# Recurrent rounds of a two-block kernel: own places for the second round's rates and keys, the next preparation inside the inverse's steps, and decays as one exponential per direction

## The chip, the cores and the metric

One core of one Trainium2 chip runs the whole program. The metric is the device time of one execution in microseconds. Three executions of the kernel before gave 1541.13 us as their median (1539.18 to 1548.11).

## What is computed

Two blocks stand behind one another. The second, two transformer layers with three kinds of attention, isn't touched. The first block mixes pooling, a gated linear recurrence (HGRN) and an RWKV recurrence. The change lies in the RWKV part, which has 6 heads of 64 channels and two directions, over 256 context and 256 latent tokens:

```python
w_log = -softplus(-(w0[d] + tanh(xw) @ w_up[d])) - 0.5
decay = exp(-exp(w_log))                       # = exp(-DECAY * sigmoid(...)), DECAY = exp(-0.5)
a  = sigmoid(a0[d] + xa @ a_up[d])
kk = k * k_k;  kk = kk * rsqrt(sum(kk * kk) + 1e-12)
k_mod = k * (1 + (a - 1) * k_a)
...
sa = S @ kk_t                                  # one step of the scan, per head
S  = S * w_t - sa * (kk_t * a_t) + v_t * k_t
y  = S @ r_t
```

## The kernel before, in words

The program is written in Bass: each engine has its own instruction list, which it carries out in order, and semaphores tie the lists together. TensorE does the matmuls into PSUM, ScalarE (ACT in the rows) and VectorE (DVE) copy results out and do the elementwise work.

The scan isn't run token by token. 6 heads are taken as 3 **rounds** (`JT` = 3) of two heads, both directions together, in 4 chunks of 128 tokens. A round j has these parts, each a Python generator that every engine's list runs through in the same order of turns:

- **E, prepare** (`prepare_tensor` L876, `prepare_scalar` L1825, `prepare_vector` L2316): products for the rates (L883, `w` then `a`) and for the norm (L887), sigmoids (L1836) into `sw` and `la`, the sigmoids of HGRN's gates (L1850, L1851), the norm by Ln and Exp (L1857, L1860). VectorE sums the rates over each chunk (the scan L2325) and makes `km` (modified keys). ScalarE makes the decays as exponentials (L1867 to L1874), VectorE multiplies them into the keys `km` and rates `la` (L2354 to L2358).
- **S, scores** (L899, L1880, L2366): transposes of values, `km`, `la`; products of `la` with the queries `px`.
- **L, full tiles** (L965, L2389): four turns, `lk0`, `lk1`, `akb0`, `akb1`. TensorE multiplies `km` and `la` with `px` and `rl` (L973, L983), VectorE copies the result out under a mask (L2396).
- **I, inverse** (L988, L1951, L2400): 12 turns, six halvings l = 1 to 6 of two turns each. The first, called i1 to i6 here, is a product (L955; L962 for i6) whose result ScalarE copies out (L2001, one copy per direction). The second, x1 to x6, is a product (L955; L962 for x6) with, up to l = 5, its transposed form t1 to t5 (L946); VectorE copies these out (L2406; L2417 and L2426 for x6).
- **C, chain** (L1019, L1962, L2430): 8 turns, chunk by chunk: products rhs (L1030, L1034) and u (L1045), each copied by ScalarE, then s (L1053 to L1057), copied by VectorE (L2438). **Y** (L1060) reads the outputs.
- **H**, 12 turns of HGRN's work; **Q** and **N** (L1095, L1080), norms of HGRN's and RWKV's outputs; **T**, the rest of the input projection, ahead of the first round; **M**, the output projection, in the last.

The order of turns is written out by hand: `TAIL` (L239) and `order_of_streams` (L242). In a round's string each E is a turn of the *next* round's preparation. It lies in the second half of the inverse (i4 to x6) and in the chain:

```python
turns += list("SSS" + "ILHIHILHIHILHIHL")
if more:
    n = "N" if j else ""
    turns += list(f"IEQ{n}IEQ{n}IEQ{n}IEIEQ{n}EQ{n}IEQ{n}" + "CECHCHECHCHECHCHC" + "Y")
```

`la` and `km` have one place each for all rounds (L496), and S and L of round j read them. So `prepare_scalar` waits at L1828 for the product `akb1` of round j-1 and at L1829 for its transposes.

PSUM banks are handed out by `Pool` (L201) in the order of turns: a product waits until the last user of its bank has been copied out. The RWKV pool has 4 banks. What matters below: t3 takes the banks of `akb0`, and x4 those of `akb1`.

Of the kernel before, what the change touches and what calls it, by code (L numbers as in the profile page):

```python
# [18 lines left out]
ALU = mybir.AluOpType  # L19
# [219 lines left out]
TAIL = "TTETETTTTTTTTETTEETEHTETEHTHTHTETHTEH"  # L239

def order_of_streams():  # L242

    turns, steps = list(TAIL), []
    for j in range(JT):
        more = j + 1 < JT
        turns += list("SSS" + "ILHIHILHIHILHIHL")
        if more:
            n = "N" if j else ""
            turns += list(f"IEQ{n}IEQ{n}IEQ{n}IEIEQ{n}EQ{n}IEQ{n}" + "CECHCHECHCHECHCHC" + "Y")  # L250
        else:
            turns += list("IQNIQNIQNIQNQNIQNIM" + "CMCMCMCMCMCMCMCM" + "YMNNMNMNNMMMMN")
# [10 lines left out]
def run_streams(**streams):  # L263
# [124 lines left out]
def build(nc, a, out, first=True, second=True, dump=None):  # L388
# [3 lines left out]
    with ctx:  # L392
        sems = {}

        def sem(name):
            if name not in sems:
                sems[name] = ctx.enter_context(nc.semaphore(name))
            return sems[name]
# [60 lines left out]
        dmid, nmid, ecol = take(8, (2, 4)), take(8, (2, 4)), take(16, (2, 2, 4))  # L459
# [37 lines left out]
        nd, n6, xh, xth = [slots[0][:, n * 1024:(n + 1) * 1024].rearrange("p (d u t) -> p d u t", d=2, t=HALF) for n in range(4)]  # L497
        xf, lkm = [slots[2][:, n * 2048:(n + 1) * 2048].rearrange("p (d u t) -> p d u t", d=2, t=P) for n in range(2)]
# [377 lines left out]
        def prepare_tensor(pe, j, take_bank, turn):  # L876
# [12 lines left out]
            for _ in range(6):  # L889
                yield  # L890
# [934 lines left out]
        def prepare_scalar(act, j, copy, done, emptied):  # L1825

            if j:
                rw.wait_filled(act, f"akb1_{j - 1}")  # L1828
                ep.wait_filled(act, f"btok1_{j - 1}")  # L1829
# [11 lines left out]
            done("e_gates")  # L1841
            yield
# [19 lines left out]
            yield  # L1862
            for d in range(2):
                act.wait_ge(sem("e_cumulated"), 2 * j + d + 1)
                for c in range(4):
                    q = slice(c * P, (c + 1) * P)
                    act.activation(sw[:, d, q], sw[:, d, q], ACT.Exp, scale=-DECAY, bias=dmid[:, d, c:c + 1])  # L1867
                    if c >= 2:
                        act.activation(pl[:, d, (c - 2) * P:(c - 1) * P], cl[:, d, q], ACT.Exp, scale=-DECAY, bias=dmid[:, d, c:c + 1])
                act.activation(ecol[:, j % 2, d], ecol[:, j % 2, d], ACT.Exp)  # L1870
                act.drain()
                for c in range(4):
                    q = slice(c * P, (c + 1) * P)
                    act.activation(cl[:, d, q], cl[:, d, q], ACT.Exp, scale=DECAY, bias=nmid[:, d, c:c + 1])  # L1874
# [441 lines left out]
        def prepare_vector(dve, j, done, emptied, bc, fence):  # L2316
# [3 lines left out]
            k = us[:, 3 + j, :]  # L2320
            for d in range(2):
# [39 lines left out]
            yield  # L2361
# [645 lines left out]
```

## Time and profile before

| | before |
|---|---|
| median of 3 executions (lowest, highest) | 1541.13 us (1539.18, 1548.11) |
| the profiled execution, its time | 1543.86 us |
| its span in the profile | 1542.1 us |
| mean granted TensorE clock | 0.98 |
| TensorE busy | 1466.3 us (95%) |
| VectorE busy | 817.6 us (53%) |
| ScalarE busy | 336.7 us (22%) |

### The profile page before, as it was taken

To read this page: it belongs to the slowest core of one execution; us is meant where nothing else is said; L and a number is where in the kernel's file an instruction comes from. 1 tells how busy PE (TensorE), PEld (TensorE's weight loads), DVE (VectorE), ACT (ScalarE), POOL (GpSimd) and SP (SyncE) were. 2 spreads that over 40 slices of the span, in tenths; PEclk is the share of its full clock that TensorE was granted. 3 is DMA by queue.
4 is the path that set the end of the run, shared out by engine and by line. 5 is a ranking of instruction groups with operands and counts; after the bars stand their busy time and mean duration, and the time that the engine had idled before them with its cause. 6 is when DMAs were issued, how large, how long until landed. Compare 5 with 4: busy or idle time off the path is not lost.

```text
span 1542.1 us, 30923 instructions
## 1 busy us (share of the span) xinstructions
PE 1466.3 (95%) x13431; PEld 1277.7 (83%) x13431; DVE 817.6 (53%) x1497; ACT 336.7 (22%) x721; POOL 279.1 (18%) x144
## 2 busy tenths in 40 slices
PE   7999998889788989999999999999999999999998
PEld 2666857777677878998888999999999888899986
DVE  2342244565653258667622766534866743466653
ACT  1103132543532231033400121001104340012100
POOL 3403001000000018663200000002875320000000
PEclk9999999989799999999999999999999999999999
DMA  9313150000003246433344454454553324345451
GB/s 352 127 55 109 57 190 2 4 2 4 17 3 112 77 108 225 164 110 110 113 161 163 142 175 175 167 164 125 179 177 143 116 110 149 130 163 172 164 188 61
DMA packets 101239, 191.30 MB, mean 124 GB/s; under 512 B 8648, under 2 KB 17568, under 8 KB 100976
## 3 DMA queue, kind: packets, MB, share of 16 engines
q1 hardware_dynamic: 99728, 187.39, 35.1%
q8 instruction: 107, 1.75, 0.5%
q0 software_dynamic: 928, 1.26, 0.3%
q10 hardware_dynamic: 448, 0.66, 0.2%
q14 instruction: 28, 0.23, 0.0%
HBM read 187.32 MB, written 1.05 MB: 122 GB/s over the span
## 4 chain that ended last, share of the span: by engine, by line
PE 82%; DVE 4%; PEld 3%; ACT 3%; issue 3%; DMA 2%; DVEq 2%; ACTq 1%; SPq 0%; PEldq 0%
PE psum L1403 16%; PE psum L1264 13%; PE psum L1239 13%; PE psum L1400 6%; PE psum L1520 3%; PE psum L1260 3%; PE psum L871 3%; PEld psum L1539 2%; PE psum L1455 2%; PE psum L955 2%; PE psum L946 2%; PE psum L1122 2%; PE psum L1539 2%; PE psum L1559 1%; PE psum L1324 1%
## 5 line engine op out<-in xcount | busy, mean ns | idle before, releaser
L1264 PE MATMUL psum<-arena 128*128 128x128 f32 x2240 | 262.6, 276 | 1.6 <-DVE arena L2600 1.0
L1264 PEld LDWEIGHTS psum<-arena 128*128 128x128 f32 x2240 | 255.3, 192 | 10.5 <-issue 8.4
L2001 ACT ACTIVATE arena<-psum 128x256 f32<-128x256 f32 (+6 forms) x244 | 115.9, 490 | 631.1 <-PE psum L1264 109.4
L1403 PEld LDWEIGHTS psum<-arena 128*128 128x128 f32 x2240 | 250.4, 192 | 0.1
L1403 PE MATMUL psum<-arena 128*128 128x128 f32 x2240 | 250.5, 274 | 0.0
L1239 PE MATMUL psum<-arena 128*128 128x256 f32 x896 | 195.7, 379 | 0.0
L1239 PEld LDWEIGHTS psum<-arena 128*128 128x128 f32 x896 | 169.3, 189 | 24.7 <-issue 0.3
L826 POOL TENSOR_TENSOR arena<-arena 128x1024 f32<-128x1024 f32 x12 | 28.4, 2369 | 524.6 <-DMA arena<-in_w_in 507.6
L1400 PE MATMUL psum<-arena 128*128 128x256 f32 x448 | 97.0, 379 | 0.0
L1400 PEld LDWEIGHTS psum<-arena 128*128 128x128 f32 x448 | 84.9, 190 | 11.9
L1539 PE MATMUL psum<-arena 128*128 128x256 f32 x336 | 73.4, 379 | 0.8 <-issue 0.8
L1539 PEld LDWEIGHTS psum<-arena 128*128 128x128 f32 x336 | 63.2, 189 | 11.8 <-issue 2.8
L2866 DVE TENSOR_TENSOR arena<-arena 128x1024 f32<-128x1024 f32 x28 | 34.3, 1225 | 64.0 <-PE psum L1400 30.8
L871 PE MATMUL psum<-arena 128*128 128x256 f32 x256 | 56.7, 379 | 3.5 <-DVE arena L2311 3.5
L1455 PE MATMUL psum<-arena 128*128 128x128 f32 (+2 forms) x331 | 48.0, 285 | 11.1 <-DMA arena<-in_c_ctx 5.0
L1520 PE MATMUL psum<-arena 128*128 128x256 f32 (+1 forms) x176 | 57.4, 484 | 0.4 <-issue 0.3
L871 PEld LDWEIGHTS psum<-arena 128*128 128x128 f32 x256 | 48.2, 189 | 10.7 <-issue 3.8
L1455 PEld LDWEIGHTS psum<-arena 128*128 128x128 f32 (+2 forms) x331 | 38.9, 149 | 19.3 <-issue 12.1
L1520 PEld LDWEIGHTS psum<-arena 128*128 128x128 f32 x176 | 33.9, 194 | 23.4 <-issue 20.6
L1260 PE MATMUL psum<-arena 128*128 128x256 f32 x224 | 49.3, 380 | 0.0
L955 PE MATMUL psum<-arena 64*64 64x64 f32 x1920 | 38.7, 223 | 9.2 <-issue 6.9
L1260 PEld LDWEIGHTS psum<-arena 128*128 128x128 f32 x224 | 42.1, 189 | 6.4 <-issue 0.7
(397 smaller groups left out, 2018.7 us busy)
## 6 DMA issues: line engine op xcount, KB each, us to landing
arena<-in_w_in SPq DMA_DIRECT2D x33, 2048.0 KB, 8.1
arena<-in_w_up SPq DMA_DIRECT2D x16, 2048.0 KB, 8.5
arena<-in_w_down SPq DMA_DIRECT2D x16, 2048.0 KB, 7.9
arena<-in_w_out SPq DMA_DIRECT2D x6, 2048.0 KB, 7.9
arena<-in_w_branch SPq DMA_DIRECT2D x6, 2048.0 KB, 7.6
arena<-in_mod_w SPq DMA_DIRECT2D x5, 2048.0 KB, 13.8
arena<-in_w_in SPq DMA_DIRECT2D x3, 1024.0 KB, 6.5
arena<-in_mod_w SPq DMA_DIRECT2D x2, 1024.0 KB, 6.5
```

Of the source, the lines that this page charges most:

```text
L871: mm = pe.matmul(b[:, i * T:(i + 1) * T], w[:, k, c0 + i * P:c0 + (i + 1) * P], raw[:, k, :], start=k == 0 and i == 0, stop=k == KT - 1, s ...
L955: mm = pe.matmul(b[out, u * HALF:(u + 1) * HALF], left(d, u, k), right(d, u, k), start=True, stop=True)
L1239: mm = pe.matmul(b[:, i * T:(i + 1) * T], w[:, k, c:c + P], src[:, k, :], start=k == 0, stop=k == ks - 1)
L1260: mm = pe.matmul(b[:, 0:T], right[:, k, :], left[:, k, :], start=k == 0, stop=k == half - 1)
L1264: mm = pe.matmul(b[:, n * P:(n + 1) * P], left[:, k, n * P:(n + 1) * P], right[:, k, :], start=k == 0, stop=k == half - 1)
L1400: mm = pe.matmul(b[:, 0:T], right[:, k, :], left[:, k, :], start=first and k == 0, stop=last and k == half - 1, skip_group_check=True)
L1403: mm = pe.matmul(b[:, n * P:(n + 1) * P], left[:, k, n * P:(n + 1) * P], right[:, k, :], start=first and n == 0 and k == 0, stop=last and ...
L1455: return pe.transpose(dst, src, ident[0:n, 0:n])
L1520: mm = pe.matmul(b[:, n0:512], w[:, k, c0:c0 + P], xt[:, k, n0:512], start=k == 0, stop=k == KT - 1)
L1539: mm = pe.matmul(b[:, n * T:(n + 1) * T], left[:, k, n * P:(n + 1) * P], right[:, k, :], start=k == 0, stop=k == half - 1)
L2001: return act.activation(dst, src, ACT.Copy, scale=scale)
L2866: dve.tensor_tensor(s1, w21, w22, ALU.add)
```

## The change

Three things are done. Round 1 gets its own `la` and `km`, in places that round 0's gate inputs, keys and values leave free, while rounds 0 and 2 keep the old ones; ScalarE's two waits are replaced by one for the last read of `sw` and `pl`. The next round's E turns begin three turns into the inverse: the products for the rates stand ahead of x1 and i2, VectorE's two sums (one per direction) ahead of `akb0` and `akb1`, and the exponentials of the decays between i5 and the chain. E has 11 turns in place of 10. The middle of each chunk, so far a bias of four exponentials of 128 columns, is subtracted on VectorE first, so that each exponential is one instruction of 512 (or 256) columns.

```diff
-TAIL = "TTETETTTTTTTTETTEETEHTETEHTHTHTETHTEH"
+TAIL = "TTETETTETETTTTTETTEETEHTETEHTHTHTETHTH"
...
-        turns += list("SSS" + "ILHIHILHIHILHIHL")
         if more:
             n = "N" if j else ""
-            turns += list(f"IEQ{n}IEQ{n}IEQ{n}IEIEQ{n}EQ{n}IEQ{n}" + "CECHCHECHCHECHCHC" + "Y")
+            turns += list("SSS" + "ILHEIHEILHIHEILHIHEL" + f"IEQ{n}IEQ{n}Q{n}IEQ{n}IEQ{n}IEQ{n}IE" + "CCHCHECHCHCHCHC" + "Y")
         else:
-            turns += list("IQNIQNIQNIQNQNIQNIM" + "CMCMCMCMCMCMCMCM" + "YMNNMNMNNMMMMN")
+            turns += list("SSS" + "ILHIHILHIHILHIHL" + "IQNIQNIQNIQNQNIQNIM" + "CMCMCMCMCMCMCMCM" + "YMNNMNMNNMMMMN")
...
+        rates, mods = [la, hz[:, 0:4:3], la], [km, us[:, 3:7:3], km]
...
             if j:
-                rw.wait_filled(act, f"akb1_{j - 1}")
-                ep.wait_filled(act, f"btok1_{j - 1}")
+                act.wait_ge(sem("s_queries"), 2 * j)
...
             for d in range(2):
                 act.wait_ge(sem("e_cumulated"), 2 * j + d + 1)
-                for c in range(4):
-                    q = slice(c * P, (c + 1) * P)
-                    act.activation(sw[:, d, q], sw[:, d, q], ACT.Exp, scale=-DECAY, bias=dmid[:, d, c:c + 1])
-                    if c >= 2:
-                        act.activation(pl[:, d, (c - 2) * P:(c - 1) * P], cl[:, d, q], ACT.Exp, scale=-DECAY, bias=dmid[:, d, c:c + 1])
+                act.activation(sw[:, d, :], sw[:, d, :], ACT.Exp, scale=-DECAY)
+                act.activation(pl[:, d, :], cl[:, d, T:2 * T], ACT.Exp, scale=-DECAY)
                 act.activation(ecol[:, j % 2, d], ecol[:, j % 2, d], ACT.Exp)
                 act.drain()
-                for c in range(4):
-                    q = slice(c * P, (c + 1) * P)
-                    act.activation(cl[:, d, q], cl[:, d, q], ACT.Exp, scale=DECAY, bias=nmid[:, d, c:c + 1])
+                act.activation(cl[:, d, :], cl[:, d, :], ACT.Exp, scale=DECAY)
...
-                dve.tensor_scalar(dmid[:, d], c[:, at::P], DECAY, None, ALU.mult)
-                dve.tensor_scalar(nmid[:, d], c[:, at::P], -DECAY, None, ALU.mult)
+                e, m = ecol[:, j % 2, d], mid[:, d]
+                dve.tensor_copy(m, c[:, at::P])
                 dve.tensor_tensor(km[:, d, :], km[:, d, :], k, ALU.mult)
                 fence()
+                dve.tensor_tensor(blocks_of(c), blocks_of(c), m.unsqueeze(2).to_broadcast([P, 4, P]), ALU.subtract)
+                fence()
                 dve.tensor_tensor(w, c, w, ALU.subtract)
```

**VectorE, middle of round 0's inverse.** Before, from the copy of `akb0` (L2396) to the scan of direction 0 (L2325); L2406 are the copies of x and t of one halving, L2563 and L2565 HGRN's output, the second L2396 is `akb1`:

```order
L2396 COPY_PREDICATED arena<-arena,psum 128x1024
L2406 COPY_PREDICATED arena<-arena,psum 128x32x8 x4
L2563 COPY arena<-psum 128x256
L2565 TENSOR_TENSOR arena<-psum,arena 128x256
L2396 COPY_PREDICATED arena<-arena,psum 128x1024
L2476 SCALAR_TENSOR_TENSOR arena<-arena 128x256
L2406 COPY_PREDICATED arena<-arena,psum 128x16x16 x4
L2325 SCALAR_TENSOR_TENSOR arena<-arena 128x512
```

In the changed kernel, from HGRN's output (now L2562, L2564) to the copies of x4 and t4 (now L2405):

```order
L2562 COPY arena<-psum 128x256
L2564 TENSOR_TENSOR arena<-psum,arena 128x256
L2323 SCALAR_TENSOR_TENSOR arena<-arena 128x512
L2324 TENSOR_SCALAR arena<-arena 128x512
L2328 COPY arena<-arena 128x4
L2329 TENSOR_TENSOR arena<-arena 128x512
L2331 TENSOR_TENSOR arena<-arena 128x512
L2333 TENSOR_TENSOR arena<-arena 128x512
L2334 TENSOR_SCALAR arena<-arena 128x4
L2339 SCALAR_TENSOR_TENSOR arena<-arena 128x2
L2340 SCALAR_TENSOR_TENSOR arena<-arena 128x1
L2395 COPY_PREDICATED arena<-arena,psum 128x1024
```

The whole sum of direction 1 (nine instructions) stands between HGRN's output and the copy of `akb1`. That of direction 0 stands in the same way ahead of the copy of `akb0`.

**ScalarE, from the copies of i5 of round 0 on.** Before, the two copies of i5, then (left out here) HGRN's gates, the copies of i6 (64x512), the norm, and the decays of direction 0 ahead of the chain's first copies (128x128 x2):

```order
L2001 ACTIVATE arena<-psum 64x512 x2
L1857 ACT_TABLE_LOAD
L1857 ACTIVATE arena<-psum,arena 128x512
L1939 ACTIVATE arena<-psum,arena 128x256
L1860 ACT_TABLE_LOAD
L1860 ACTIVATE arena<-arena 128x512
L1942 ACTIVATE arena<-arena 128x256
L1867 ACTIVATE arena<-arena 128x128 x3
```

The same norm and decays in the changed kernel:

```order
L1998 ACTIVATE arena<-psum 128x512 x2
L1860 ACT_TABLE_LOAD
L1860 ACTIVATE arena<-psum,arena 128x512
L1936 ACTIVATE arena<-psum,arena 128x256
L1863 ACT_TABLE_LOAD
L1863 ACTIVATE arena<-arena 128x512
L1867 ACTIVATE arena<-arena 128x512
L1868 ACTIVATE arena<-arena 128x256
L1869 ACTIVATE arena<-arena 128x4
L1871 ACTIVATE arena<-arena 128x512
L1939 ACTIVATE arena<-arena 128x256
L1998 ACTIVATE arena<-psum 64x512 x2
```

The norm and the decays of direction 0 now stand between the copies of i5 (128x512 x2) and those of i6 (64x512 x2). The decays of direction 1 follow behind the copies of i6, ahead of the chain.

## Rows read from the trace of the kernel before

**Rows 1.** Windows: us busy per engine (and count), granted clock, DMA share, GB/s.

```profile
300.00:320.00 20.00, 13.88 (x121) 13.12 (x117) 15.40 (x34) 14.38 (x36) 0.00 (x0) 0.60 0.00 1
390.00:410.00 20.00, 11.26 (x134) 10.63 (x131) 14.95 (x33) 14.09 (x36) 0.00 (x0) 0.65 0.10 31
409.00:417.00 8.00, 8.00 (x64) 7.30 (x63) 5.94 (x14) 1.86 (x4) 0.00 (x0) 0.53 0.01 3
```

**Rows 2.** Chain of waits, round 0: start, us, what the end hung on.

```profile
303.06 1.30 ACTq L1858
```

**Rows 3.** Timeline of ScalarE: start, us, instruction, [idle before]; rounds 0 and 1.

```profile
296.24 1.09 ACT L2001 ACTIVATE arena<-psum 128x512 f32<-128x512 f32 x2 [1.79 <-PE psum L955]
...
307.71 0.42 ACT L1942 ACTIVATE arena<-arena 128x256 f32<-128x256 f32 x1
308.23 0.99 ACT L1867 ACTIVATE arena<-arena 128x128 f32<-128x128 f32 x3
...
311.64 0.45 ACT L2001 ACTIVATE arena<-psum 128x128 f32<-128x128 f32 x2
...
384.77 1.09 ACT L2001 ACTIVATE arena<-psum 128x512 f32<-128x512 f32 x2 [1.29 <-PE psum L955]
```

**Rows 4.** Timeline of TensorE: x4, the products of E, then round 2's x6 and u.

```profile
288.72 1.16 PE L955 MATMUL psum<-arena 64*64 64x64 f32 x64 [0.27 <-ACT arena L2001]
...
292.05 1.13 PE L883 MATMUL psum<-arena 64*128 64x512 f32 x4 [0.32 <-ACT arena L1836]
294.01 1.10 PE L887 MATMUL psum<-arena 128*128 128x512 f32 x2 [0.83 <-ACT arena L1836]
...
377.55 1.16 PE L955 MATMUL psum<-arena 64*64 64x64 f32 x64
...
486.91 2.31 PE L962 MATMUL psum<-arena 64*64 64x64 f32 x32 [0.83 <-ACT arena L2001]
...
494.34 1.00 PE L1045 MATMUL psum<-arena 128*128 128x64 f32 x8
```

**Rows 5.** Timeline of VectorE: copies of akb0 and akb1, rounds 0 and 1.

```profile
278.68 1.35 DVE L2396 COPY_PREDICATED arena<-arena,psum 128x1024 f32<-128x1024 int32 x1 [2.42 <-PE psum L983]
...
286.35 1.35 DVE L2396 COPY_PREDICATED arena<-arena,psum 128x1024 f32<-128x1024 int32 x1 [0.16 <-PE psum L983]
...
367.39 1.35 DVE L2396 COPY_PREDICATED arena<-arena,psum 128x1024 f32<-128x1024 int32 x1 [1.76 <-PE psum L983]
...
374.88 1.35 DVE L2396 COPY_PREDICATED arena<-arena,psum 128x1024 f32<-128x1024 int32 x1 [0.16 <-PE psum L983]
```

**Rows 6.** Timeline of VectorE: first and last of one direction's sum, and a key.

```profile
294.51 1.23 DVE L2325 TENSOR_TENSOR_SCAN arena<-arena 128x512 f32<-128x512 f32 x1 [2.30 <-ACTq L2004]
...
298.00 0.17 DVE L2339 TENSOR_TENSOR arena<-arena 128x3 f32<-128x3 f32 x1
...
315.35 0.69 DVE L2354 TENSOR_TENSOR arena<-arena 128x512 f32<-128x512 f32 x1
```

**Rows 7.** Timeline of VectorE: copies of the chain's s, and round 2's x6 (L2426).

```profile
317.56 0.61 DVE L2438 SCALAR_TENSOR_TENSOR arena<-psum,arena 128x128 f32<-128x128 f32 x2
...
325.28 0.35 DVE L2438 SCALAR_TENSOR_TENSOR arena<-psum,arena 128x128 f32<-128x128 f32 x1 [0.32 <-PE psum L1057]
...
409.34 0.61 DVE L2438 SCALAR_TENSOR_TENSOR arena<-psum,arena 128x128 f32<-128x128 f32 x2
...
418.51 0.35 DVE L2438 SCALAR_TENSOR_TENSOR arena<-psum,arena 128x128 f32<-128x128 f32 x1 [0.32 <-PE psum L1057]
...
489.64 0.69 DVE L2426 COPY arena<-psum 64x512 f32<-64x512 f32 x1
...
495.87 0.80 DVE L2438 SCALAR_TENSOR_TENSOR arena<-psum,arena 128x128 f32<-128x128 f32 x2 [4.94 <-PE psum L1057]
```

**Rows 8.** Windows around a gap of TensorE in round 2 (columns as in rows 1).

```profile
475.00:478.00 3.00, 0.40 (x22) 0.26 (x14) 1.40 (x3) 0.00 (x0) 0.00 (x0) 0.98 0.59 218
478.00:481.00 3.00, 2.74 (x47) 2.44 (x47) 0.00 (x0) 1.32 (x3) 0.00 (x0) 0.50 0.04 9
```

More of the change, by code:

```diff
@@ L458, in build @@
         pos_i = take(T).bitcast(I32)
-        dmid, nmid, ecol = take(8, (2, 4)), take(8, (2, 4)), take(16, (2, 2, 4))
+        mid, ecol = take(8, (2, 4)), take(16, (2, 2, 4))
         share = top[0]
@@ L888, in prepare_tensor @@
             yield
-            for _ in range(6):
+            for _ in range(8):
                 yield
@@ L896, in prepare_tensor @@
             yield
-            yield
         def score_tensor(pe, j, take_bank, turn):
+            la, km = rates[j], mods[j]
             b = take_bank(ep, f"vtok_{j}")
@@ L965, in full_tensor @@
         def full_tensor(pe, j, take_bank, turn):
+            la, km = rates[j], mods[j]
             for d in range(2):
@@ L1825, in prepare_scalar @@
         def prepare_scalar(act, j, copy, done, emptied):
+            la = rates[j]
             if j:
-                rw.wait_filled(act, f"akb1_{j - 1}")
-                ep.wait_filled(act, f"btok1_{j - 1}")
+                act.wait_ge(sem("s_queries"), 2 * j)
             act.activation(rn, us[:, 3 + j, :], ACT.Square, scale=rc[:, j, 0:1])
@@ L1841, in prepare_scalar @@
             done("e_gates")
+            yield
+            yield
             yield
@@ L2320, in prepare_vector @@
             k = us[:, 3 + j, :]
+            la, km = rates[j], mods[j]
             for d in range(2):
@@ L2328, in prepare_vector @@
                 at = HALF - 1 + d
-                dve.tensor_scalar(dmid[:, d], c[:, at::P], DECAY, None, ALU.mult)
-                dve.tensor_scalar(nmid[:, d], c[:, at::P], -DECAY, None, ALU.mult)
+                e, m = ecol[:, j % 2, d], mid[:, d]
+                dve.tensor_copy(m, c[:, at::P])
                 dve.tensor_tensor(km[:, d, :], km[:, d, :], k, ALU.mult)
                 fence()
+                dve.tensor_tensor(blocks_of(c), blocks_of(c), m.unsqueeze(2).to_broadcast([P, 4, P]), ALU.subtract)
+                fence()
                 dve.tensor_tensor(w, c, w, ALU.subtract)
-                last = c[:, (0 if d else P - 1)::P]
-                e, m = ecol[:, j % 2, d], dmid[:, d]
-                dve.scalar_tensor_tensor(e, last, -DECAY, m, ALU.mult, ALU.add)
+                dve.tensor_scalar(e, c[:, (0 if d else P - 1)::P], -DECAY, None, ALU.mult)
                 fence()
                 if d == 0:
-                    dve.tensor_tensor(e[:, 0:3], e[:, 0:3], m[:, 1:4], ALU.subtract)
+                    dve.scalar_tensor_tensor(e[:, 0:3], m[:, 1:4], -DECAY, e[:, 0:3], ALU.mult, ALU.add)
                 else:
-                    dve.tensor_tensor(e[:, 1::2], e[:, 1::2], m[:, 0::2], ALU.subtract)
-                    dve.tensor_tensor(e[:, 0:1], e[:, 0:1], m[:, 3:4], ALU.subtract)
+                    dve.scalar_tensor_tensor(e[:, 1::2], m[:, 0::2], -DECAY, e[:, 1::2], ALU.mult, ALU.add)
+                    dve.scalar_tensor_tensor(e[:, 0:1], m[:, 3:4], -DECAY, e[:, 0:1], ALU.mult, ALU.add)
                 done("e_cumulated")
                 yield
+            yield
+            yield
             yield
@@ L2360, in prepare_vector @@
                 yield
-            yield
             ep.wait_filled(dve, f"bonus_{j}")
```

1 line of the change is left out of this document (removed), and 2 rows, old and new, of the table GROUPS.

## Prediction

> **What bounds the kernel now.** I began with the busy shares by stretch. TensorE is nearly always busy except in two places, the end of the inverse and the first chunk of the chain in rounds 0 and 1 [rows 1]: there it is busy for 13.9 and 11.3 of 20 us, and much of that at a granted clock of 0.50, while VectorE and ScalarE are busy for 14 to 15. The chain of waits says what ends last there: in round 0 it runs over ScalarE's table load for the norm [rows 2] and on through the decays. ScalarE's own timeline shows why the chain of chunks stands still: its first copies start at 311.64, behind the eleven instructions that make direction 0's decays [rows 3], and VectorE's copies of the chain's first s end at 317.56 + 0.61 = 318.17 in round 0 and at 409.95 in round 1 [rows 7]. In round 2, which prepares nothing, u begins at 494.34 and the copies of s end at 496.67, 2.3 us later [rows 4, 7]. So there is a stall to win, some 8 to 10 us a round. The question is what the moved work costs where it goes: the first half of the inverse, where TensorE has hardly a gap. I follow three marks in each round: the start of x4 (288.72, 377.55), the end of the copies of i5 (296.24 + 1.09 = 297.33, and 385.86), and the end of the copies of s (318.17, 409.95) [rows 3, 4, 7].
>
> **Up to x4: three delays.** First, the products of E. Before, they stand behind x4 or fill the gap ahead of it; now they stand in a stretch in which TensorE is the bound. L883 twice and L887 once take 1.13 + 1.13 + 1.10, and with the 0.83 us for which L887 waits for a bank [rows 4] this makes 4.2, less 0.1 of overlap: **+4.1**. Second, the sum of direction 0 on VectorE now precedes the copy of `akb0`. From scan to last instruction it takes 294.51 to 298.17, 3.7 with its semaphore; the new subtraction is one more instruction like L2354, 0.69, with its fence [rows 6]: 4.4 in all. VectorE was idle for 2.42 us ahead of that copy [rows 5], which hides so much, so t3, which needs the banks of `akb0`, is late by **+2.0**; in round 1 the idle time is 1.76, so +2.65. Third, the sum of direction 1 precedes the copy of `akb1`. Here VectorE was idle for only 0.16 us. The copy ended at 287.70 and x4, which takes those banks, began at 288.72 [rows 4, 5], so 1.0 of the 4.4 is hidden: **+3.4**. In round 1 the copy ended at 376.23 and x4 began at 377.55, 1.3 hidden: +3.1. x4 is thus late by 9.5 in round 0 and by 9.9 in round 1.
>
> **From x4 to the copies of i5: a gain.** Before, 3.3 us lay between the end of t4 (292.05 less 0.32) and the end of L887 [rows 4]. In their place comes the product of HGRN's norm, half the columns of L887, an estimate of 0.65. The gates on ScalarE fit beside x4 and t4. Round 0 gains 2.6. Round 1 takes a second such product for RWKV's norm: 8.3 (377.55 to 385.86) becomes 6.6, a gain of 1.7.
>
> **From there to s: the gain that is meant.** Before, 318.17 - 297.33 = 20.8 us. Now ScalarE does, behind i5's copies, what it did from 303.06 to 308.23 [rows 2, 3], 5.2 us, with the decays of direction 0 added. These took 308.23 to 311.64, 3.4 us, in eleven instructions; now they are four. By L1942, an exponential of 256 columns at 0.42, I take two of 512 at 0.6, one of 256 at 0.4, and 0.3 for the small one and the drain: 1.9. The copies of i6 (1.2) then end 8.3 us behind those of i5. x6 and VectorE's copies of it took 486.91 to 490.33, 3.4 us [rows 4, 7]: u can start at 11.8. VectorE then owes the keys of direction 1, three instructions of 0.69 with fences, 2.1, and the copies of s, 0.6: 14.6. TensorE's own way, 2.3 at full clock and up to 4.2 at half, ends at 14.1 to 16.0. I take 15.3, a gain of **5.5** (4.8 to 6.2). Round 1 has two more small instructions on ScalarE and three on VectorE for RWKV's norm: 16.7 in place of 24.1, a gain of **7.4**.
>
> The table loads deserve a word. In the rows one starts at 303.06 and what follows it starts 1.30 us later [rows 2]; the drain behind it costs nothing that can be seen. The Trainium skill (ScalarE: Activation LUTs, section "What ACT_TABLE_LOAD costs") gives 2.66 us for each switch of set, a drain included. By it the two switches that now stand between i5 and i6 would add 2.7 us a round. The trace disagrees, and its value is the one in the sum.
>
> **The clock.** TensorE will now wait for about 4.8 us ahead of x4: 2.2 us of `akb1` and i4 are done while VectorE needs 0.95 for HGRN's output, 4.4 for the sum and 1.35 for the copy. In round 2 the clock was at 0.50 right after a gap of this kind (3 us with 0.40 busy) [rows 8]. x4 and t4, some 3 us of work, would then lose up to 1.7. Between 0 and 1.7 I take 0.85 a round, +1.7 in all. Against it, the half clock that now follows s in round 1 may go: from the copies of the first s to those of the second it is 8.9 us there (409.95 to 418.86) and 7.5 in round 0 (318.17 to 325.63) [rows 1, 7]. Of this 1.4 I take half, -0.7.
>
> **The sum.** Round 0: 9.5 - 2.6 - 5.5 = +1.4. Round 1: 9.9 - 1.7 - 7.4 = +0.8. Clock: +1.7 - 0.7. Together +3.2 us. The preparation of round 0 lies beside the input projection, which TensorE bounds, and I cost it at nothing (0.4 us at most); its cover is the stretch of products in which VectorE is mostly idle. ScalarE's removed wait by itself is worth nothing here, since what it guards is long done where E now stands in round 0; it is what lets E be put ahead of `akb1` at all. The profiled execution took 1543.86 us, so 1547.1 by its own time; that execution is 2.7 above the median, and by the median of 1541.13 I say **1544.5 us**. A change of 0.5% is 7.7 us, about what this measurement can tell from none.
>
> **The rivals.**
> - **The sums hide after all, and it is faster** (0.25). The delays of `akb0` and `akb1` (2.0 + 3.4 + 2.65 + 3.1 = 11.2) rest on VectorE running late exactly where a bank is reused. If HGRN's output on TensorE, itself late by 4.1, leaves gaps in which VectorE works ahead, or if x4 is held by something else, they shrink; with them the clock's 1.7 goes. It decides by whether the copy of `akb1` ends before ScalarE's copies of i4. For it: VectorE is idle for some 2 us before each of several copies. Against it: 0.16 us ahead of `akb1` [rows 5]. All of it gone gives 3.2 - 11.2 - 1.7 = -9.7, 1531.4 us.
> - **Half clock from x4 to the second chunk, and it is slower** (0.15). A gap ahead of x4, one ahead of x6 (2 to 3 us) and those of the first chunk come close behind one another, and the clock doesn't recover between them, as it did not from 409 to 416 although TensorE was busy all the time [rows 1]. Then x4 to i5 lose 4.7 in place of 0.85, x5 to i6, partly beside ScalarE, 1.4, and x6 to the second s about 1.7: 7 a round, 1544.5 + 14 = 1558.5 us. The Trainium skill (TensorE: Matmul & The Clock Gate, "What's actually happening") says that the throttled state is the default and activity releases it, which speaks for this.
> - **Table switches at their full price** (0.05): if the drain behind a switch does hold i6's copies now that they follow it, another 2.7 a round, 1550 us. This is the mechanism that the page above would give; rows 2 are against it.
> - **The overlap changes nothing** (0.12): the preparation could begin where it did, the path through norm, decays and keys stays as long as before, and stalls only change places: 1541 us.
> - My forecast, a small loss of up to 7 us (0.43).
>
> **Range and chances.** From 1531 (the faster case in full) to 1554 (between the forecast's upper bound, 3.2 + 2.4 for the clock and half clock in the chain, and the half-clock case); it leaves out some 0.08 below and 0.12 above. Faster by over 0.5% (under 1533.4) takes most of the first rival and the forecast's lower edge: 0.23. Slower by over 0.5% (above 1548.8) takes the half-clock case, the table case and the forecast's upper edge: 0.25. The rest, 0.52, is within 0.5%.
>
> **What would show it.** In the changed profile: x4 waits some 5 us for VectorE's copy of `akb1` (right if the idle time before x4 names that copy, wrong if it is under 1 us); i6's copies end about 8 us behind i5's; u starts 12 us behind them; the decays of a direction take 1.9 us; and from the copies of i5 to those of s it is 15 to 17 us. The clock should show 0.50 right behind the gap ahead of x4. I am wrong if the start of x4 comes less than 5 us later than before in its round, or if the stretch from x4 to s shrinks by much more than 8 to 9 us.

## The result, and the profile after

The changed kernel takes **1563.51 us** (median of 4, 1560.91 to 1566.62), beside 1540.92 us (1539.18 to 1548.11) for the kernel before on the same chip: a ratio of **1.0146**, 95% interval 1.0128 to 1.0164. It is 22.6 us slower, outside the forecast's range. Its profiled execution took 1562.71 us, span 1560.9, mean clock 0.978.

The loss has two parts. The first is in a place that the forecast had costed at nothing. The page's group of the seven-product projection shows it; the columns are busy time and mean ns of one, then the idle time ahead of them and what ended most of it. Before:

```profile
L1539 PE MATMUL psum<-arena 128*128 128x256 f32 x336 | 73.4, 379 | 0.8 <-issue 0.8
```

After:

```profile
L1540 PE MATMUL psum<-arena 128*128 128x256 f32 x336 | 75.5, 386 | 11.5 <-DVE arena L2197 10.7
```

TensorE's timeline of the changed kernel has the whole wait in one place:

```profile
137.45 14.09 PE L1540 MATMUL psum<-arena 128*128 128x256 f32 x64 [0.26 <-issue]
162.25 12.45 PE L1540 MATMUL psum<-arena 128*128 128x256 f32 x48 [10.71 <-DVE arena L2197]
```

L2197 is VectorE's first copy of this projection's products. VectorE's timeline shows what stands ahead of it: both sums of round 0's preparation, which the new `TAIL` puts there.

```profile
144.73 1.22 DVE L2323 TENSOR_TENSOR_SCAN arena<-arena 128x512 f32<-128x512 f32 x1
...
147.31 2.68 DVE L2331 TENSOR_TENSOR arena<-arena 128x512 f32<-128x512 f32 x1
150.06 2.33 DVE L2333 TENSOR_TENSOR arena<-arena 128x512 f32<-128x512 f32 x1
152.32 2.30 DVE L2334 TENSOR_SCALAR arena<-arena 128x4 f32<-128x4 f32 x1
154.69 0.16 DVE L2337 SCALAR_TENSOR_TENSOR arena<-arena 128x3 f32<-128x3 f32 x1
154.97 3.22 DVE L2323 TENSOR_TENSOR_SCAN arena<-arena 128x512 f32<-128x512 f32 x1
158.11 0.52 DVE L2324 TENSOR_SCALAR arena<-arena 128x512 f32<-128x512 f32 x1
...
161.23 0.15 DVE L2340 SCALAR_TENSOR_TENSOR arena<-arena 128x1 f32<-128x1 f32 x1
161.50 0.69 DVE L2197 COPY arena<-psum 128x512 f32<-128x512 f32 x1
```

Two things are to be seen. The copy that frees TensorE's banks waits for both sums, and the sums are slow themselves: an instruction on 128x4 elements takes 2.30 us, the same one 0.16 later on. GpSimd's timeline shows what runs beside them, its sums of a projection's weights:

```profile
146.53 2.90 POOL L800 TENSOR_TENSOR arena<-arena 128x1024 f32<-128x1024 f32 x1 [14.12 <-DMA arena<-in_w_in]
149.58 2.26 POOL L802 TENSOR_TENSOR arena<-arena 128x1024 f32<-128x1024 f32 x1
151.81 2.78 POOL L803 TENSOR_TENSOR arena<-arena 128x1024 f32<-128x1024 f32 x1
154.77 2.34 POOL L805 TENSOR_TENSOR arena<-arena 128x1024 f32<-128x1024 f32 x1 [0.18 <-issue]
```

Each slow VectorE instruction ends within its own usual length of the end of a GpSimd one: L2334 at 154.62, L803 at 154.59; the two subtractions of 0.69 us 0.6 behind L800 and L802; the scan at 158.19, 1.1 behind GpSimd's last, 157.11. So the sums take 16.7 us in place of 9 (no_gpsimd_sums below).

The second part is in the rounds. This is TensorE's timeline of round 0, then the waits of round 1 for the same banks and for x6. Before, x4 waited 0.27 us [rows 4].

```profile
295.45 3.54 PE L946 MATMUL psum<-arena 64*64 64x64 f32 x64 [2.81 <-DVE arena L2395]
...
309.09 1.84 PE L955 MATMUL psum<-arena 64*64 64x64 f32 x64 [4.99 <-DVE arena L2395]
...
316.70 1.16 PE L955 MATMUL psum<-arena 64*64 64x64 f32 x64 [1.32 <-ACT arena L1998]
...
324.78 3.28 PE L962 MATMUL psum<-arena 64*64 64x64 f32 x32 [3.25 <-ACT arena L1998]
...
390.32 2.96 PE L946 MATMUL psum<-arena 64*64 64x64 f32 x64 [2.85 <-DVE arena L2395]
...
403.95 1.99 PE L955 MATMUL psum<-arena 64*64 64x64 f32 x64 [4.35 <-DVE arena L2395]
...
422.40 3.27 PE L962 MATMUL psum<-arena 64*64 64x64 f32 x32 [4.63 <-ACT arena L1998]
```

t3 waits for the copy of `akb0`, x4 for that of `akb1`, x6 for ScalarE's copies of i6. The chain of waits runs over the second sum of round 0 straight into x4:

```profile
302.98 1.23 DVE arena L2323
304.21 0.44 DVEq L2325
...
304.89 0.60 DVEq L2330
...
305.56 0.69 DVE arena L2331
...
306.33 0.69 DVE arena L2333
...
307.53 1.32 DVE arena L2395
...
309.09 1.84 PE psum L955 x64
```

The windows (columns as in [rows 1]) show what each wait does to the clock: right behind the one ahead of t3, and for 12 us behind the one ahead of x6, it is at 0.50, the lower of its two levels (1.2 in place of 2.4 GHz).

```profile
294.00:296.00 2.00, 0.55 (x12) 0.55 (x14) 1.90 (x3) 0.00 (x0) 0.00 (x0) 0.92 0.03 8
296.00:298.00 2.00, 2.00 (x42) 2.00 (x42) 0.46 (x2) 0.00 (x0) 0.00 (x0) 0.50 0.00 0
...
322.00:324.00 2.00, 0.00 (x0) 0.00 (x0) 1.83 (x4) 1.73 (x5) 0.00 (x0) 0.74 0.00 0
324.00:336.00 12.00, 11.22 (x69) 11.13 (x70) 9.05 (x20) 4.03 (x11) 0.00 (x0) 0.50 0.00 1
```

Where the span grew, read from the first product of S of each round (L922), one execution each:

| start of round | before | after | grown by |
|---|---|---|---|
| 0 | 254.25 | 265.13 | 10.9 |
| 1 | 344.37 | 360.32 | 15.9 |
| 2 | 437.61 | 457.23 | 19.6 |

Up to the start of round 0 it is 10.9, in round 0 5.1 and in round 1 3.7; behind round 2's start nothing more is lost (the span grew by 18.8).

### The profile page after: what moved, and what is told of

The parts are those of the page before. It is cut to its first block, busy times and chain, and to the rows that moved or that the text cites. A ratio compares the mean times of both kernels' runs of the same rounds, so it can differ in the third digit from the quotient of the medians.

```text
span 1560.9 us, 30885 instructions
## 1 busy us (share of the span) xinstructions
PE 1470.1 (94%) x13431; PEld 1282.5 (82%) x13431; DVE 829.1 (53%) x1497; ACT 327.9 (21%) x679; POOL 280.2 (18%) x144
## 4 chain that ended last, share of the span: by engine, by line
PE 83%; DVE 5%; DMA 2%; DVEq 2%; issue 2%; ACT 2%; PEld 2%; ACTq 1%; SPq 0%; PEldq 0%
PE psum L1404 16%; PE psum L1265 14%; PE psum L1240 12%; PE psum L1401 6%; PE psum L1521 4%; PE psum L1261 3%; PE psum L871 3%; PE psum L1456 2%; PE psum L946 2%; PE psum L1560 2%; PE psum L955 2%; PEld psum L1540 2%; PE psum L1123 2%; PE psum L1540 2%; PE psum L1325 1%
## 5 line engine op out<-in xcount | busy, mean ns | idle before, releaser
L1265 PEld LDWEIGHTS psum<-arena 128*128 128x128 f32 x2240 | 254.3, 192 | 11.6 <-issue 8.0
L1404 PEld LDWEIGHTS psum<-arena 128*128 128x128 f32 x2240 | 250.4, 192 | 0.1
L1240 PE MATMUL psum<-arena 128*128 128x256 f32 x896 | 195.7, 379 | 0.0
L1240 PEld LDWEIGHTS psum<-arena 128*128 128x128 f32 x896 | 169.2, 189 | 24.7 <-issue 0.3
L1401 PE MATMUL psum<-arena 128*128 128x256 f32 x448 | 97.0, 379 | 0.0
L1401 PEld LDWEIGHTS psum<-arena 128*128 128x128 f32 x448 | 84.8, 190 | 11.9
L1540 PE MATMUL psum<-arena 128*128 128x256 f32 x336 | 75.5, 386 | 11.5 <-DVE arena L2197 10.7
L1540 PEld LDWEIGHTS psum<-arena 128*128 128x128 f32 x336 | 64.5, 193 | 23.3 <-DVE arena L2197 11.1
L871 PE MATMUL psum<-arena 128*128 128x256 f32 x256 | 56.7, 378 | 3.5 <-DVE arena L2308 3.5
L1456 PE MATMUL psum<-arena 128*128 128x128 f32 (+2 forms) x331 | 47.7, 284 | 10.9 <-DMA arena<-in_c_ctx 4.8
L871 PEld LDWEIGHTS psum<-arena 128*128 128x128 f32 x256 | 48.2, 189 | 10.7 <-issue 3.8
L955 PE MATMUL psum<-arena 64*64 64x64 f32 x1920 | 39.4, 232 | 17.3 <-DVE arena L2395 9.3
L955 PEld LDWEIGHTS psum<-arena 64*64 64x64 f32 x1920 | 34.9, 144 | 24.7 <-issue 18.2
L1456 PEld LDWEIGHTS psum<-arena 128*128 128x128 f32 (+2 forms) x331 | 38.8, 149 | 19.0 <-issue 11.8
L1521 PEld LDWEIGHTS psum<-arena 128*128 128x128 f32 x176 | 33.9, 195 | 23.5 <-issue 20.6
L946 PE MATMUL psum<-arena 64*64 64x64 f32 x1152 | 42.5, 235 | 8.3 <-DVE arena L2395 5.7
```

The lines of the kernel that those rows point to most:

```text
L871: mm = pe.matmul(b[:, i * T:(i + 1) * T], w[:, k, c0 + i * P:c0 + (i + 1) * P], raw[:, k, :], start=k == 0 and i == 0, stop=k == KT - 1, s ...
L946: mm = pe.matmul(b[o, u * HALF:(u + 1) * HALF], left(u, r), right[r, u, :], start=True, stop=True)
L955: mm = pe.matmul(b[out, u * HALF:(u + 1) * HALF], left(d, u, k), right(d, u, k), start=True, stop=True)
L1240: mm = pe.matmul(b[:, i * T:(i + 1) * T], w[:, k, c:c + P], src[:, k, :], start=k == 0, stop=k == ks - 1)
L1265: mm = pe.matmul(b[:, n * P:(n + 1) * P], left[:, k, n * P:(n + 1) * P], right[:, k, :], start=k == 0, stop=k == half - 1)
L1401: mm = pe.matmul(b[:, 0:T], right[:, k, :], left[:, k, :], start=first and k == 0, stop=last and k == half - 1, skip_group_check=True)
```

## The experiments

Below, "two rounds" is the time from the start of round 0 to that of round 2 in the profiled execution: 183.4 us before, 192.1 in the changed kernel. Where two kernels are compared, so are their ratios to the kernel before, each timed beside it.

### The tail: the sums behind the projection's first copies

**tail_late.** The changed kernel, with the two sums again where they stood before, behind the first copies of the projection.

```diff
-TAIL = "TTETETTETETTTTTETTEETEHTETEHTHTHTETHTH"
+TAIL = "TTETETTTTTTTTETTEEEETEHTETEHTHTHTETHTH"
```

> The changed kernel with one edit: in the order ahead of round 0 the two turns that hold VectorE's sums of the rates go back behind the first seven-product projection (the string of turns alone is changed). Theory (the sums stand ahead of the copies of those products, TensorE fills its four banks and waits 10.7 us): the wait is gone, x4 of round 0 comes 9.5 us later than in the kernel before instead of 20.4, and the time falls by 10.9 us to about 1552.5. Rival (the 10.9 us would be lost later anyway, the rounds being bound by something else that is late as well): the time stays within 3 us of 1563.5.

Measured: 1551.19 us, ratio 1.0055 (1.0032 to 1.0077). TensorE's timeline has no wait in the projection any more, and the waits in the rounds stay:

```profile
138.84 24.46 PE L1540 MATMUL psum<-arena 128*128 128x256 f32 x112 [0.26 <-issue]
...
283.57 3.48 PE L946 MATMUL psum<-arena 64*64 64x64 f32 x64 [3.27 <-DVE arena L2395]
...
297.09 1.98 PE L955 MATMUL psum<-arena 64*64 64x64 f32 x64 [4.98 <-DVE arena L2395]
```

Round 0 starts at 253.80. So the string `TAIL` alone costs 12 us by the medians, 14 by the ratios, and the two rounds take 191.3, nearly as in the changed kernel (192.1). The wait is not the whole of the price. From their start to that of the next group these 112 instructions take 24.7 us here (138.84 to 163.56) and 37.5 in the changed kernel (137.45 to 174.96). Of the 12.8 more, 10.7 are the wait and 2.1 the half clock behind it: the granted clock fell to 0.50 while TensorE waited, and stayed there for about 3.7 us of its work.

**tail_one_early.** As tail_late, with direction 0's sum ahead of the copies and direction 1's behind.

```diff
-TAIL = "TTETETTTTTTTTETTEEEETEHTETEHTHTHTETHTH"
+TAIL = "TTETETTETTTTTTTTEEEETEHTETEHTHTHTETHTH"
```

> As tail_late, but the sum of direction 0 stays ahead of the first projection's copies, the one of direction 1 goes behind them. Theory A (queue alone: a sum takes 4.5 us as in the rounds): VectorE is free at about 149.2, before TensorE has filled its fourth bank at 151.5, so nothing is lost against tail_late, 1552.5. Theory B (queue and GpSimd: VectorE's instructions take 2.3 to 3.2 us instead of 0.16 to 1.2 while GpSimd sums weights from 146.5 to 157): the sum ends at about 154.8, TensorE waits 4 us, 1556.5.

Measured: 1555.97 us, ratio 1.0089 (1.0064 to 1.0114), 4.8 us by the medians above tail_late, as theory B has it. TensorE's timeline:

```profile
156.15 13.29 PE L1540 MATMUL psum<-arena 128*128 128x256 f32 x48 [4.19 <-DVE arena L2197]
```

One sum makes TensorE wait for 4.2 us, two for 10.7: VectorE had some 6 us of slack ahead of this copy (16.7 less 10.7; here the sum and its fence take 10.2 us, less 4.2).

**no_gpsimd_sums.** The changed kernel without the four GpSimd instructions that stand beside VectorE's sums. It leaves the sums of those weights out, so the products there are made with unsummed weights.

```diff
                     w11, w21, w12, w22 = quarters(ring[:, SLOT[n]])
+                    if i == 2:
+                        gp.drain().then_inc(sem("first_weights_summed"), 1)
+                        gp.drain().then_inc(sem("first_weights_summed"), 1)
+                        continue
```

> The changed kernel as it is (both sums ahead of the first seven-product projection), without GpSimd's four sums of the third such projection's weights (L800 to L805, from 146.53 to 157.11 in the changed kernel), so its products use unsummed weights. Theory A (VectorE and GpSimd can't work at once there: each of VectorE's instructions waits until GpSimd's is done): VectorE's two sums take 9 us in place of 16.7, the first copy L2197 starts at about 154 in place of 161.50, TensorE's wait for it falls from 10.7 to 3 or 4 us, and the kernel takes 1555 to 1557 us. Theory B (the sums are slow for another reason, such as the long queue of TensorE's copies or the clock of TensorE): they take 15 us or more and the time stays at 1563.

Measured: 1552.22 us, ratio 1.0066 (1.0042 to 1.0089). Four lines were added, so all line numbers behind them are 4 higher. VectorE's timeline, and then TensorE's:

```profile
146.77 0.69 DVE L2337 TENSOR_TENSOR arena<-arena 128x512 f32<-128x512 f32 x1
147.38 0.16 DVE L2338 TENSOR_SCALAR arena<-arena 128x4 f32<-128x4 f32 x1
...
147.90 1.22 DVE L2327 TENSOR_TENSOR_SCAN arena<-arena 128x512 f32<-128x512 f32 x1
...
152.43 0.69 DVE L2201 COPY arena<-psum 128x512 f32<-128x512 f32 x1
```

```profile
153.18 12.27 PE L1544 MATMUL psum<-arena 128*128 128x256 f32 x48 [2.96 <-DVE arena L2201]
```

The same instructions take 0.69, 0.16 and 1.22 again, the two sums from 143.43 to 152.3, 8.9 us, and TensorE's wait falls from 10.7 to 3.0. The sums' place alone makes TensorE wait for 3.0 us; the other 7.7 of the wait come from VectorE and GpSimd working against each other. The Trainium skill (SBUF — State Buffer, section "SBUF: two separate sides") says that VectorE, when it has two inputs in SBUF or runs in a two-port mode, and GpSimd share a pair of ports that the one which starts first holds for its whole instruction. The trace agrees with its 2.30 us for 128x4 elements, which end with GpSimd's instruction.

Not every instruction of VectorE is held. In the kernel before, where these turns hold copies out of PSUM, with at most one input in SBUF, they keep their length beside the same GpSimd instructions; VectorE's line first, then GpSimd's:

```profile
149.53 0.69 DVE L2204 TENSOR_TENSOR arena<-psum,arena 128x512 f32<-128x512 f32 x1 [1.90 <-PE psum L1539]
```

```profile
148.80 2.35 POOL L800 TENSOR_TENSOR arena<-arena 128x1024 f32<-128x1024 f32 x1 [14.92 <-DMA arena<-in_w_in]
```

The time fell by more than I expected, 11.3 us by the medians in place of 7; the start of round 0 is 9.2 earlier (255.93), of which 1.3 lie ahead of the projection, and the rest is within the scatter of the runs.

### The rounds: the sums behind the copies

**sums_behind_copies.** tail_late, and in each round the sum of direction 0 behind the copy of `akb0`, that of direction 1 behind the copy of `akb1`.

```diff
-"ILHEIHEILHIHEILHIHEL"
+"ILHEIHEILHIHILEHIHLE"
```

> tail_late with a second edit: in a round the sum of direction 0 stands behind the copy of akb0 and that of direction 1 behind the copy of akb1, not ahead of them. Theory (what costs is the bank that the late copy holds, for t3 and for x4): TensorE's waits of 2.8 and 5 us for these copies go, and with them the half clock behind them (t3 3.5 us, t4 3.0 us instead of 2.0): 2.0 + 2.65 for t3, 2.7 + 2.4 for x4, 3 to 5 for the clock, together 12 to 15 us below tail_late, about 1539. Rival (VectorE has too much to do in this stretch, so the sums delay the copies of x3 and x4 by as much): no more than 3 us below tail_late, 1549 or more.

Measured: **1533.12 us**, ratio **0.9949** (0.9932 to 0.9966): faster than the kernel before, by 0.5% or some 8 us. The two rounds take 176.3. TensorE's timeline has no wait for the copies of `akb0` and `akb1`; what is left in round 0 is one for ScalarE's copies of i4 ahead of x4, one for VectorE's copies of t4 ahead of i5, and one for ScalarE ahead of x6:

```profile
288.37 1.16 PE L955 MATMUL psum<-arena 64*64 64x64 f32 x64 [1.33 <-ACT arena L1998]
...
293.68 1.16 PE L955 MATMUL psum<-arena 64*64 64x64 f32 x64 [1.67 <-DVE arena L2405]
...
304.24 3.12 PE L962 MATMUL psum<-arena 64*64 64x64 f32 x32 [3.09 <-ACT arena L1998]
```

In round 1 a longer wait has come up ahead of i5, for a step of RWKV's norm on VectorE (L2456). It stands behind the second sum and the copies of x4 and t4, and x5 and t5 run at half clock behind it (1.98 and 2.99 us, 1.16 and 1.89 in round 0):

```profile
381.93 0.70 PE L1090 MATMUL psum<-arena 128*128 128x256 f32 x2 [2.84 <-DVE arena L2456]
```

No run puts this step ahead of the second sum.

**sum1_early.** The same, with the sum of direction 1 ahead of the copy of `akb1` again.

```diff
-"ILHEIHEILHIHILEHIHLE"
+"ILHEIHEILHIHILEHIHEL"
```

> The order of sums_behind_copies, but with the sum of direction 1 ahead of the copy of akb1 again; the sum of direction 0 stays behind the copy of akb0. Theory A (each sum costs what its copy is late: 18 us for the two in both rounds, some 40% of it by the first): the wait of x4 for L2395 comes back with 4 to 5 us, that of t3 does not; 4.5 to 5.5 us a round, 1541 to 1544 us. Theory B (the two delays cost only together, because the first makes the second late and halves the clock for both): under 3 us a round, below 1538 us.

Measured: 1542.54 us, ratio 0.9999 (0.9986 to 1.0012), 0.5% or 7.7 us over sums_behind_copies; two rounds 184.6, 8.3 more. Theory A, a little under its range: each sum has its own price, 4.1 us a round for this one, and the one ahead of `akb0` has the rest of the 15.0 between tail_late and sums_behind_copies, 3.4 a round.

**sum1_behind_x4.** The sum of direction 1 one step later than in sums_behind_copies, behind VectorE's copies of x4 and t4.

```diff
-"ILHEIHEILHIHILEHIHLE" + f"IEQ{n}IEQ{n}Q{n}...
+"ILHEIHEILHIHILEHIHL" + f"IQ{n}IEEEQ{n}Q{n}...
```

> The order of sums_behind_copies, with the sum of direction 1 one step later still: behind VectorE's copies of x4 and t4, which i5 waits for (1.67 us in round 0 on L2405); ScalarE's gates of HGRN then both stand behind the step of x4. Theory A (VectorE, not TensorE, sets the start of i5 in round 0): that wait goes, and the kernel is 1 to 2 us faster than sums_behind_copies, 1530 to 1532 us. Theory B (the sum of direction 1 is then late for ScalarE's decays, or the copies of x5 wait behind it): no gain or a loss of up to 2 us.

Measured: 1535.54 us, ratio 0.9942 (0.9927 to 0.9957). Theory B: nothing that can be told from sums_behind_copies. Round 0 took 84.5 in place of 86.5, round 1 92.4 in place of 89.8.

**sum1_by_round.** That order in round 0, the other in round 1.

```diff
+("ILHEIHEILHIHILEHIHLE" if j else "ILHEIHEILHIHILEHIHL")
+(f"IEQ{n}IEQ{n}Q{n}..." if j else f"IQ{n}IEEEQ{n}Q{n}...")
```

> sum1_behind_x4's order in round 0 (84.5 us from start to start, against 86.5 in sums_behind_copies) and sums_behind_copies' in round 1 (89.8 against 92.4). Theory A (the differences of the rounds are real): 2 us faster than sums_behind_copies, 1531 us. Theory B (they are the scatter of one execution): 1533 to 1535 us.

Measured: 1533.54 us, ratio 0.9942 (0.9922 to 0.9962), two rounds 175.8. Theory B again. Round 0 took 84.2 us, as in sum1_behind_x4, but round 1 took 91.6 in the order that had taken 89.8 in sums_behind_copies: in one execution's marks, 2 us of a round is too little to go by.

### The rest of the change

**products_twice.** sums_behind_copies with the products of the next preparation issued twice, which leaves the result as it is.

```diff
+                    if j:
+                        pe.matmul(bs[d], w[r, j * P:(j + 1) * P], src[r, :], start=True, stop=True)
                     pe.matmul(bs[d], w[r, j * P:(j + 1) * P], src[r, :], start=True, stop=True).then_inc(ep.filled, 1)
...
+            if j:
+                pe.matmul(kb, cst("blocks"), rn, start=True, stop=True)
```

> The order of sums_behind_copies, with the products of the next preparation (w, a, kk: L883 twice, L887 once, 3.4 us) issued twice in rounds 0 and 1. Theory A (TensorE bounds the first half of the inverse, so that the products moved there cost their full duration, as the prediction has it with +4.1 a round): +3.3 us a round, x4 starts 3.3 us later behind the start of the round, 1538 us. Theory B (ScalarE's and VectorE's copies set the pace there and part of the products fits beside them): +1.5 us a round or less, under 1535 us.

Measured: 1535.45 us, ratio 0.9944 (0.9925 to 0.9963); two rounds 180.1, 3.8 more. For about 3.1 us of products x4 starts 2.5 us later in round 0 (38.3 us behind the start of the round in place of 35.8) and 1.0 later in round 1 (37.4 in place of 36.4). What is left at the end of a round, 1.3 and 2.5 us, is mixed with the clock: in round 0 x6 also starts 2.5 later, but takes 2.10 us in place of 3.12, because the clock falls later, and in round 1 it takes 3.28 in place of 1.87.

```profile
305.34 2.10 PE L967 MATMUL psum<-arena 64*64 64x64 f32 x32 [2.34 <-ACT arena L2003]
```

Neither theory holds as it stood. TensorE pays for most of a product there in round 0 and for a third of it in round 1. By the ratios this kernel is 0.8 us faster than sums_behind_copies, with an interval of some 4 either way, so the 6.6 of theory A is out.

**decays_alone.** The kernel before, with nothing changed but the exponentials: one per array and direction.

```diff
-                for c in range(4):
-                    q = slice(c * P, (c + 1) * P)
-                    act.activation(sw[:, d, q], sw[:, d, q], ACT.Exp, scale=-DECAY, bias=dmid[:, d, c:c + 1])
...
+                act.activation(sw[:, d, :], sw[:, d, :], ACT.Exp, scale=-DECAY)
+                act.activation(pl[:, d, :], cl[:, d, T:2 * T], ACT.Exp, scale=-DECAY)
```

> The kernel before with the exponentials of the changed kernel alone: one instruction of 512 (or 256) columns per exponential, the middle of the chunk subtracted on VectorE; order and places as before. Theory A (ScalarE's chain of norm and decays sets the end of the first chunk, as the chain of waits says): 1.5 us less per direction on that chain, 3 us per round, two rounds, 1535. Theory B (VectorE sets it: from e_norm at 307.6 it works without a gap until the copies of s at 318.2): nothing is won, 1541, within 1.5 us.

Measured: 1544.54 us, ratio 1.0025 (1.0007 to 1.0043). Theory B, and a little worse: 0.25% slower than the kernel before, where no difference was expected. ScalarE is done earlier and nothing comes of it. The copies of the first s of round 0 end at 318.46 (318.17 before), because VectorE works without a gap from the norm to there. The two rounds take 186.7, 3.3 more. In round 0 the start of s is 0.5 us later in its round and the round 1.6 longer; behind s the half clock lasts longer (L894 takes 2.07 us in place of 1.13).

**old_decays_behind.** The other way round: sums_behind_copies with the old four-fold exponentials and without the subtraction.

> The order of sums_behind_copies (profiled 1531.7 us), with the four exponentials per array and direction of the kernel before in place of one. Theory A (ScalarE's decays now stand ahead of the copies of i6, which TensorE waits for, 3.1 and 2.7 us in rounds 0 and 1): direction 0's decays take 3.4 us again in place of 1.8, x6 starts 1.5 us later, and the keys of direction 1 follow later too; 2 to 3 us a round, the kernel is 4 to 6 us slower than sums_behind_copies, 1537 to 1539 us. Theory B (VectorE sets the end of the stretch, as in decays_alone, where nothing was won): within 2 us of it.

Measured: 1534.76 us, ratio 0.9937 (0.9922 to 0.9953); two rounds 178.2. Theory B. TensorE's wait ahead of x6 is longer, as theory A has it, but it starts earlier, and x6 comes 52.4 us behind the start of round 0, in place of 51.7; in round 1 it is 55.7 in both. Round 0:

```profile
303.46 3.27 PE L962 MATMUL psum<-arena 64*64 64x64 f32 x32 [4.83 <-ACT arena L2003]
```

What the single exponential saves ScalarE (3.4 to 1.8 us a direction), the subtraction takes from VectorE (0.7 of its own, on the path through the sums).

**decays_behind_i6.** sums_behind_copies, with the norm's exponential and direction 0's decays behind ScalarE's copies of i6.

```diff
-...IEQ{n}Q{n}IEQ{n}IEQ{n}IEQ{n}IE"
+...IEQ{n}Q{n}IEQ{n}IQ{n}IEQ{n}IEE"
```

> The order of sums_behind_copies (1533.1 us), with the step of the norm's exponential and direction 0's decays one place later, behind ScalarE's copies of i6, and the keys of both directions behind VectorE's copies of x6. Theory A (ScalarE's work ahead of the copies of i6 sets the end of the stretch): x6 waits for under 1.5 us in place of 3.1 and 2.7, and it is 1 to 2 us a round faster, 1529 to 1532 us. Theory B (VectorE's own sum of work, norm, keys and copies, sets it, as decays_alone and old_decays_behind showed): what x6 wins is waited for again by the copies of s, and the time is within 1.5 us of 1533 or up to 3 slower.

Measured: 1537.26 us, ratio 0.9971 (0.9950 to 0.9991). The wait ahead of x6 is gone, 0.83 in place of 3.09, and TensorE waits behind it instead; TensorE's timeline:

```profile
300.95 1.87 PE L962 MATMUL psum<-arena 64*64 64x64 f32 x32 [0.83 <-ACT arena L1998]
...
305.45 1.08 PE L1046 MATMUL psum<-arena 128*128 128x64 f32 x4 [1.60 <-ACT arena L1998]
...
314.45 1.13 PE L1143 MATMUL psum<-arena 64*64 64x64 f32 x32 [1.67 <-DVEq L2914]
```

Theory B: what x6 wins is waited for again behind it. By the ratios this order is 0.2% slower than sums_behind_copies, within the intervals of the two.

## Why the prediction was wrong

**The step that failed is the last of its sum**: "The preparation of round 0 lies beside the input projection … its cover is the stretch of products in which VectorE is mostly idle", costed at nothing. It cost 12 us by the medians (1563.51 to 1551.19), more than half of the loss: 10.7 of waiting and 2.1 of half clock behind it. VectorE was idle for most of that stretch, and still the cover was none: what counts is whether the moved work stands ahead of a copy that frees a bank. The forecast asked this question for `akb0` and `akb1`, of an order written in the same turns, and didn't ask it of `TAIL`. Nor did it look at what GpSimd does in that stretch, which made the sums nearly twice as long and the wait 7.7 us longer. Without this step the forecast of 1544.5 meets the 1551.2 of tail_late: inside the range, but a loss of 0.55% where 0.2% was forecast, so the rounds were mis-sized too. (The sum as written gives 1541.13 + 3.2 = 1544.3.)

**Up to x4: the total right, by two errors that cancel.** x4 is late by 9.5 (43.96 from the round's start in place of 34.47) and 10.4 us; the forecast was 9.5 and 9.9. In sums_behind_copies, where the sums are out of the way, it is late by only 1.4 and 3.2. So the moved products cost 1.4 and 3.2, not **+4.1**: part of them falls into gaps of 0.3 to 1.0 us that TensorE had in the first half before, of which the largest in round 0 was this, in its timeline:

```profile
269.05 1.02 PE L955 MATMUL psum<-arena 64*64 64x64 f32 x50 [1.04 <-issue]
```

And the two sums cost 8.1 and 7.2, not 5.4 and 5.8: behind the wait for `akb0` t3 runs at half clock (3.54 us in round 0, 2.26 before), which the clock term had left out.

**From x4 to i5: the gain of 2.6 and 1.7 was 1.2 and -0.8.** x4 and t4 ran at half clock, as foreseen, but beyond the 0.85 that I had taken: from the start of x4 to the end of t4 it took 4.6 and 5.0 us in place of 3.0, so 1.6 and 2.0. In round 1 a wait of 0.58 us for RWKV's norm (L2456) came on top.

**From i5 to s: 3.5 and 5.7 for 5.5 and 7.4.** i6's copies end 8.1 us behind i5's (8.3 forecast), and the decays take 1.83 (1.9). Both table loads took 1.28 us in ScalarE's rows, and the next activation starts 0.02 us behind them. So the 2.66 us that the Trainium skill (ScalarE: Activation LUTs, section "What ACT_TABLE_LOAD costs") gives with a drain don't show here, and the third rival is out. Of the 2.0 and 1.7 us that were missing the most lies in x6, 3.28 us at half clock where it takes 1.87 with only 0.83 of waiting ahead of it (decays_behind_i6). u starts 13.3 us behind i5's copies, forecast 11.8; the copies of s end 17.4 and 18.4 us behind them, outside the 15 to 17 named as the sign.

**The clock was the under-sized term.** The three waits of a round (2.8, 5.0, 3.3 us in round 0) are each followed by half clock. Against the same products at full clock, t3 loses 1.3 us (0.9 in round 1), x4 and t4 1.6 (2.0), and x6 1.4 in both: some 4.3 us a round, where the term had 0.85. The half-clock rival said 7 a round, from a clock that doesn't recover between the gaps. It did recover: x5 and t5 took 1.16 and 1.89 us, at a granted clock of 1.00. Its size was right in part, its mechanism not. The half clock behind the first s did shrink, as said: from there to the next round, round 1 is 1.9 us shorter than before, forecast 0.7.

**The first rival came near its number in part by luck.** It said that without the delays of `akb0` and `akb1` the change wins 9.7 us, 1531.4. With the sums behind these copies it is 1533.1, some 8 us won, 7.1 by the marks of one execution. That these delays decide is shown. But the rival's other terms were off both ways: x4 is late by 1.4 and 3.2 us in place of 4.1, from x4 to i5 the gain is 1.0 and -1.6 in place of 2.6 and 1.7, and from i5 to s 3.6 and 6.4 in place of 5.5 and 7.4. It was also wrong in thinking that the delays would go by themselves.

**What the parts are worth.** The overlap, set right, with the own places that it needs, brings the 0.5%: old_decays_behind has these two alone. The single exponentials bring nothing in the new order (0.9937 without them, 0.9949 with them) and cost 0.25% in the old one (decays_alone). The own places can't be judged alone: to undo them under the new order would bring back a wait on products that come later in TensorE's list, and this wasn't tried.

**Left open.** Which part of the remaining waits ahead of i5 and x6 can be won: three orders that moved work there all came out within 1533 to 1537 us. The longest one ahead of i5, 2.84 us in round 1 for RWKV's norm, was not tried by itself.

## What to carry to other kernels

Where engines run in a written order of turns, a moved step is costed by what stands behind it in its engine's list: find the next copy that frees a bank and look at how long it was idle ahead of that copy, in every place that the change touches, the start-up too. An engine that is idle on average gives no cover for an instruction put ahead of the one copy that TensorE waits for; put the moved work directly behind that copy. And before VectorE's work is moved into a quiet stretch, look whether GpSimd works there. To a wait of TensorE add the half clock behind it: 1 to 3 us each time here.

## What the runs showed of the hardware

- VectorE and GpSimd: beside GpSimd's tensor-tensor instructions of 128x1024 (2.0 to 2.4 us alone) a VectorE subtraction of 128x512 took 2.33 and 2.68 in place of 0.69, a 128x4 instruction 2.30 in place of 0.16, a scan 3.22 in place of 1.22; GpSimd's own took 2.90, 2.26 and 2.78 in place of 2.35, 2.00 and 2.35. Without GpSimd's the VectorE times are back (no_gpsimd_sums). VectorE's instructions of 128x512 out of PSUM kept their 0.69 us beside them (the kernel before).
- The clock: in the changed kernel TensorE was idle for 2.8 us ahead of t3, and the granted clock fell in the first microsecond of t3 (0.83 from 295 to 296, 0.50 from 296 on), though TensorE had been busy before the wait. Behind the wait ahead of x6 it stayed at 0.50 for 12 us in which TensorE was busy for 11.2. It need not fall so soon: in round 1 of sums_behind_copies x6 ran at full clock behind 2.74 us of idling, and the clock fell some 2 us after it had started.

```profile
394.73 1.87 PE L962 MATMUL psum<-arena 64*64 64x64 f32 x32 [2.74 <-ACT arena L1998]
```

- Table loads: 1.28 us each, with the next activation starting 0.02 us behind them.
